# Expert loop of a two-block transformer kernel: the two high down passes as one 512-column matmul, its halves added by ScalarE and VectorE, and operand tiles placed 32 bytes apart modulo 64

## The chip, the cores and the metric

The kernel runs on one NeuronCore of a Trainium2 chip. The metric is the device time of one execution in microseconds (us). Three runs of the kernel before gave a median of 2825.68 us (2825.58 to 2825.96).

## What is computed

The reference is a network of two hybrid layers (recurrent, attention and state space mixers, then a product-key expert layer) followed by two layers of a second kind (retention, gating, cross attention, gated feed-forward). There are 256 tokens of width 1024. The change is mostly about the expert layer:

```python
def expert_block(args):
    xb, ib, gb = args
    a = jnp.einsum('thkd,td->thk', down[ib], xb).astype(jnp.float32)
    c = (gb * jax.nn.gelu(a)).astype(up.dtype)
    return jnp.einsum('thk,thkd->td', c, up[ib]).astype(x.dtype)
```

Each token picks 16 of 16384 experts for each of 8 heads. The kernel doesn't gather them: it multiplies all tokens with all experts' `down` rows, applies gelu, multiplies by a gate matrix that is zero where an expert isn't picked, and multiplies the result with all `up` rows.

## The kernel before

Products are made from float32 values in `float32r` form: each operand is split into a high part (a ScalarE copy that rounds) and a low part (VectorE: value minus high part), and a product is three passes on TensorE, high by high, high by low, low by high. A matmul takes a stationary operand of 128x128 and a moving operand of 128x256 or 128x512.

The experts of a layer are worked in 64 blocks of 256. For the first 32 ("held") blocks the activations are computed early (L1480 and L1462) and their output products are made in one long run (L1525). The other 32 blocks go through the expert loop: `pe.loop("peer", 15)` with two blocks in a turn (b = 0 and 1), and one block ahead of the loop and one behind it. Two layers make 64 calls of each function below.

- `act_in_parts(b)` (L1537) is the down product of a block: for 2 halves `j` of 128 experts and 8 slices `kc` of the width, three matmuls of 256 columns: (`down_hi`, `h_t_expert`), (`down_hi`, `h_t_lo`), (`down_lo`, `h_t_expert`), all into PSUM bank 4 + b, `j` in its left or right half. The `down` part is stationary and the token part moves. 48 matmuls a call.
- ScalarE's `gelu(b)` (L1173) reads that bank and writes the tile `gelu`. VectorE's `coef` (L2059) multiplies by the gates, ScalarE's `coef_high` (L1176) and VectorE's `coef_low` (L2063) split the product.
- `out_of_parts(b)` (L1547) is the up product: 24 matmuls of 512 columns; `coef` parts are stationary, `up` parts move.
- In the order of their queues, ScalarE does gelu, `down_hi` (L1134), `coef_hi`, `up_hi` (L1134); VectorE does `coef`, `coef_lo`, `down_lo` (L2030), `up_lo` (L2030). SyncE loads the next blocks into `ring` when `down_lo` and `up_lo` have been made.

TensorE's order in a turn is down product of block 1, up product of block 0, down product of block 0, up product of block 1. A down product of b waits for `down_lo` and for the last `gelu` of b (the bank is free then); an up product waits for `up_lo` and `coef_lo`. Behind the loop of a layer the last down product is followed by 18 matmuls of block 0 (`out_before`), and then `out_last` waits for `coef_lo_last1`. Ahead of the loop two down products follow each other, and the first up product waits for `coef_lo0`.

Other matmuls that the change touches by where their operands lie: L598 and L1480 and L2648 (256 columns), L607, L2666 and L2925 (512 columns). In the second block's L2666 the parts of a weight tile (`w_hi`, `ring_lo`) move and those of an activation (`h_t_hi` and `h_t_lo`, `ff_hi` and `ff_lo`, `mt_hi` and `mt_lo`) are stationary, in the order (hi, hi), (activation hi, weight lo), (activation lo, weight hi). By its loops L607 has 480 matmuls of 512 columns (five blocks of columns, 48 each, in two layers), L2925 has 192, and L2666 has 64 with `mt` in each of its three passes beside those with `h_t` and `ff`.

**Where tiles lie.** Tiles are allocated one behind another in each partition, so their places follow from their sizes. `x_res`, `h_t_lo`, `ring_lo` (over `ring`) and `h_t_expert` start at a multiple of 64 bytes. `hybrid_params` has 72 words (288 bytes), so every tile behind it, with all other matmul operands (`out_hi`, `out_lo`, `coef_hi`, `coef_lo`, `held_hi`, `held_lo`, `down_*`, `up_*`, `w_hi`, `ff_*`, `mt_*`, `h_t_hi`, `lead_x_*`), starts 32 bytes past one. Matmul operands start within a tile at steps of 512 bytes, so this is a property of the tile. Below, "at 0" and "at 32" name the two places, and two operands are "apart" if one is at 0 and the other at 32.

Of the kernel before, what the change touches and what calls it, by code (L numbers as in the profile page):

```python
# [8 lines left out]
ALU = mybir.AluOpType  # L9
ACT = mybir.ActivationFunctionType  # L10
AX = mybir.AxisListType
F32 = mybir.dt.float32
# [9 lines left out]
KD = D // P  # L22
DEPTH = 2
# [29 lines left out]
HELD = BLOCKS // 2  # L53
REACH = [(0, 0, 1, 16), (16, 1, 3, 8), (40, 4, 4, 4), (56, 8, 8, 1)]
# [278 lines left out]
def build(nc, dram, out, steps):  # L333
    ctx = ExitStack()
    with ctx:
# [19 lines left out]
        with nc.sbuf_tensor("h_t_expert", [P, KD, T], F32R) as HT_EXPERT:  # L355
            pass
# [12 lines left out]
        with ExitStack() as second:  # L369
            second.enter_context(nc.sbuf_tensor("before_ya", [P, 3 * 512], F32))  # L370
# [3 lines left out]
        KEYS = sb("keys", [P, P])  # L374
        with nc.sbuf_tensor("out_lo", [P, OUT_SLOTS, D], F32R) as OUT_LO:
            pass
# [8 lines left out]
        with nc.sbuf_tensor("arena", [P, 32768 + STAGES * GROUP * 64], F32) as ARENA:  # L385
            pass

        with ExitStack() as second:
# [6 lines left out]
            over("before_w", [P, 2 * KD * T], F32)  # L395
            W_HI = over("w_hi", [P, HI_SLOTS, CHUNK_SIZE])
            FF_HI, FF_LO = over("ff_hi", [P, KF, T]), over("ff_lo", [P, KF, T])
# [5 lines left out]
        with nc.sbuf_tensor("before_gate_hi", [P, 17 * 512], F32), nc.sbuf_tensor("gate_hi0", [P, D], F32R) as GATE_HI0, \  # L403
                nc.sbuf_tensor("lead_x_hi", [P, KD, T], F32R) as LEAD_X_HI, nc.sbuf_tensor("lead_x_lo", [P, KD, T], F32R) as LEAD_X_LO, \
                nc.sbuf_tensor("first_hi", [P, 2, D], F32R) as FIRST_HI:
            pass
        DOWN_HI, DOWN_LO = sb("down_hi", [P, 2, 2 * D], F32R), sb("down_lo", [P, 2, 2 * D], F32R)
        UP_HI, UP_LO = sb("up_hi", [P, 2, 2 * D], F32R), sb("up_lo", [P, 2, 2 * D], F32R)
        with nc.sbuf_tensor("held_hi", [P, HELD_SLOTS, 512], F32R) as HELD_HI:
            pass  # L410
        with nc.sbuf_tensor("gate_hi1", [P, D], F32R) as GATE_HI1, nc.sbuf_tensor("gate_hi2", [P, D], F32R) as GATE_HI2:
            pass
# [70 lines left out]
        for n in (8, 8, 4, 2, 2):  # L483
# [12 lines left out]
            after_scr, N_SPAR, KD * T, KD * T, KD * T, TT * D, HI_SLOTS * CHUNK_SIZE, N_Z3, 2 * T, TT * 1536,  # L496
# [212 lines left out]
        def late_stage(n):  # L709

            return 32768 + (n % STAGES if n >= STAGES else n - STAGES) * GROUP * 64
# [193 lines left out]
        def hybrid_scalar(a, l):  # L905
# [274 lines left out]
            with a.loop("peer", BLOCKS // 4 - 1):  # L1180
                a.e.wait_ge(*a.at("act_in0", back=1))
                a.e.wait_ge(*a.at("coef_lo0", back=1))
                gelu(0, "gelu0")
# [9 lines left out]
                a.e.wait_ge(*a.at("coef_lo1", back=1))  # L1193
                gelu(1, "gelu1")
# [9 lines left out]
            a.e.wait_ge(*a.at("coef_lo0"))  # L1204
            gelu(0, "gelu_last0")
# [7 lines left out]
            a.e.wait_ge(*a.at("coef_lo1"))  # L1213
            gelu(1, "gelu_last1")
# [3 lines left out]
        def hybrid_tensor(pe, l):  # L1218
# [249 lines left out]
            def passes_quarter(b, q):  # L1468
# [7 lines left out]
                for kc in range(4 * first, 4 * first + 4):  # L1476
                    o = slice(kc * P, (kc + 1) * P)
                    x_hi, x_lo = (LEAD_X_HI, LEAD_X_LO) if b < OWN_X else (HT_EXPERT, HT_LO)
# [1964 lines left out]
```

## Time and profile before

| | |
|---|---|
| median of 3 runs | 2825.68 us |
| the profiled execution | 2825.48 us |
| its span, first to last instruction | 2823.7 us |
| TensorE busy | 2803.2 us, 99% |
| weight loads busy | 2528.1 us, 90% |
| VectorE, ScalarE, GpSimd busy | 69%, 50%, 5% |
| granted TensorE clock | 0.999 of full speed |

Span and time differ by 1.8 us. A matmul's own duration in the profile overlaps with the next one's, because matmuls are pipelined; what a stream of them costs is the distance from start to start, or the length of a piece of the chain over its count.

### The profile page before, as it was taken

What the parts mean: (1) busy time and instruction counts of PE and PEld (TensorE: products, weight loads), DVE (VectorE), ACT (ScalarE), POOL (GpSimd) and SP (SyncE); (2) the same over time, 40 slices, a digit from 0 to 9 for tenths busy, and PEclk for the clock granted to TensorE, in tenths of its full rate; (3) what the DMA queues carried; (4) which work ended last, traced back from release to release, by engine and by line L of the source; (5) the groups of instructions that cost most, each with busy time, mean ns of one, the idle gap of its engine ahead of it and who ended that gap; (6) DMA issues with size and microseconds to landing.
All of it is one profiled execution on the core that took longest, in us unless ns stands there. A gap on an engine that the chain in (4) does not pass through costs nothing.

```text
span 2823.7 us, 45734 instructions
## 1 busy us (share of the span) xinstructions
PE 2803.2 (99%) x18566; PEld 2528.1 (90%) x18566; DVE 1943.8 (69%) x2882; ACT 1419.7 (50%) x1707; POOL 148.4 (5%) x145
## 2 busy tenths in 40 slices
PE   8999999999999999999999999999999999999998
PEld 7899998899999889999889999988899988888997
DVE  7889888655555788988865555576656556565664
ACT  6653554544444665355454444455455444545543
POOL 0033110000000003311000000000000000000000
PEclk9999999999999999999999999999999999999999
DMA  6344666855553534466685555465555656554663
GB/s 214 124 162 138 218 247 208 287 213 199 186 194 141 187 120 158 141 217 239 205 288 215 194 192 193 149 223 170 181 166 182 187 188 185 171 180 155 175 187 133
DMA packets 219570, 530.21 MB, mean 188 GB/s; under 512 B 13546, under 2 KB 87440, under 8 KB 208400
## 3 DMA queue, kind: packets, MB, share of 16 engines
q1 hardware_dynamic: 212944, 504.32, 54.2%
q0 software_dynamic: 6464, 23.61, 2.1%
q8 instruction: 116, 1.90, 0.3%
q14 instruction: 46, 0.38, 0.1%
HBM read 507.81 MB, written 20.06 MB: 187 GB/s over the span
## 4 chain that ended last, share of the span: by engine, by line
PE 98%; DVE 1%; DMA 1%; issue 0%; ACT 0%; SPq 0%; DVEq 0%
PE ps L2666 17%; PE ps L2648 13%; PE ps L1537 13%; PE ps L1547 12%; PE ps L1525 12%; PE ps L1480 11%; PE ps L607 4%; PE ps L598 4%; PE ps L1451 2%; PE ps L2925 2%; PE ps L1462 1%; PE ps L1255 1%; PE ps L2834 0%; PE ps L2818 0%; DMA ring<-in_peer_down 0%; PE ps L1367 0%
## 5 line engine op out<-in xcount | busy, mean ns | idle before, releaser
L2267 DVE TENSOR_TENSOR ring_lo<-ring,w_hi 128x1024 fp32r<-128x1024 f32 x320 | 388.2, 1224 | 243.0 <-ACT w_hi L2263 241.7
L2263 ACT ACTIVATE w_hi<-ring 128x1024 fp32r<-128x1024 f32 x320 | 335.2, 1056 | 236.1 <-PE ps L2666 169.0
L1537 PE MATMUL ps<-h_t_lo,down_hi 128*128 128x256 f32 x1024 | 288.2, 281 | 0.0
L1537 PE MATMUL ps<-h_t_expert,down_lo 128*128 128x256 f32 x1024 | 287.8, 281 | 0.0
L1537 PE MATMUL ps<-h_t_expert,down_hi 128*128 128x256 f32 x1024 | 286.8, 280 | 0.0
L2648 PE MATMUL ps<-h_t_lo,w_hi 128*128 128x256 f32 x928 | 260.7, 281 | 0.0
L2648 PE MATMUL ps<-h_t_hi,w_hi 128*128 128x256 f32 x928 | 259.4, 280 | 0.1
L2648 PE MATMUL ps<-h_t_hi,ring_lo 128*128 128x256 f32 x928 | 259.0, 279 | 0.0
L1143 ACT ACTIVATE out_hi<-ring 128x1024 fp32r<-128x1024 f32 x128 | 135.7, 1060 | 162.0 <-PE ps L1525 154.6
L2030 DVE TENSOR_TENSOR up_lo<-ring,up_hi 128x2048 fp32r<-128x2048 f32 x64 | 146.7, 2292 | 97.7 <-ACT up_hi L1134 97.7
L2023 DVE TENSOR_TENSOR out_lo<-ring,out_hi 128x1024 fp32r<-128x1024 f32 x128 | 156.6, 1224 | 77.1 <-ACT out_hi L1143 77.1
L1547 PE MATMUL ps<-up_hi,coef_hi 128*128 128x512 f32 x512 | 200.6, 392 | 0.0
L1547 PE MATMUL ps<-up_hi,coef_lo 128*128 128x512 f32 x512 | 199.9, 390 | 0.0
L1547 PE MATMUL ps<-up_lo,coef_hi 128*128 128x512 f32 x512 | 199.4, 390 | 0.0
L1525 PE MATMUL ps<-out_hi,held_hi 128*128 128x512 f32 x512 | 199.4, 389 | 0.0
L1525 PE MATMUL ps<-out_hi,held_lo 128*128 128x512 f32 x512 | 199.2, 389 | 0.0
L1525 PE MATMUL ps<-out_lo,held_hi 128*128 128x512 f32 x512 | 199.2, 389 | 0.0
L1134 ACT ACTIVATE up_hi<-ring 128x2048 fp32r<-128x2048 f32 x64 | 122.7, 1917 | 150.5 <-PE ps L1547 147.2
L1537 PEld LDWEIGHTS ps<-h_t_lo,down_hi 128*128 128x128 f32 x1024 | 193.0, 188 | 2.4
L1537 PEld LDWEIGHTS ps<-h_t_expert,down_hi 128*128 128x128 f32 x1024 | 192.5, 188 | 2.4
L1537 PEld LDWEIGHTS ps<-h_t_expert,down_lo 128*128 128x128 f32 x1024 | 193.3, 189 | 0.0
L2666 PE MATMUL ps<-w_hi,h_t_hi 128*128 128x512 f32 x448 | 180.3, 403 | 0.4 <-DVE ring_lo L2267 0.4
(532 smaller groups left out, 7403.5 us busy)
## 6 DMA issues: line engine op xcount, KB each, us to landing
ring<-in_peer_down SPq DMA_DIRECT2D x128, 1024.0 KB, 5.6
ring<-in_w_in SPq DMA_DIRECT2D x140, 512.0 KB, 3.7
ring<-in_peer_up SPq DMA_DIRECT2D x66, 1024.0 KB, 4.8
ring<-in_w SPq DMA_DIRECT2D x132, 512.0 KB, 3.8
ring<-in_peer_up SPq DMA_DIRECT2D x124, 512.0 KB, 4.2
late_gates<-arena POOLq DMA_DIRECT2D x64, 256.0 KB, 5.2
arena<-late_gates SPq DMA_DIRECT2D x16, 1024.0 KB, 6.4
ring<-in_w_out SPq DMA_DIRECT2D x16, 512.0 KB, 4.1
```

Of the source, the lines that this page charges most:

```text
L1134: a.e.activation(to[:, slot, :], raw(which, slot), ACT.Copy).then_inc(*a.count(name))
L1143: a.e.activation(OUT_HI[:, out_slot(b, j), :], up_raw(b, j), ACT.Copy).then_inc(*a.count(f"up_hi{b}{j}"))
L1480: m = pe.e.matmul(PS[:, act_bank(b), j * T:(j + 1) * T], w[:, o], x[:, kc, :], start=kc == 0 and n == 0, stop=kc == KD - 1 and n == 2)
L1525: m = pe.e.matmul(PS[:, 2 * t + half, :], x, w, start=b == 0 and j == 0 and n == 0, stop=False, skip_group_check=True)
L1537: m = pe.e.matmul(PS[:, 4 + b, j * T:(j + 1) * T], w[:, b, o], x[:, kc, :], start=kc == 0 and n == 0, stop=kc == KD - 1 and n == 2)
L1547: m = pe.e.matmul(PS[:, 2 * t + half, :], x[:, b, c], w[:, b, o], start=False, stop=last and n == 2, skip_group_check=True)
L2023: v.e.tensor_tensor(OUT_LO[:, out_slot(b, j), :], up_raw(b, j), OUT_HI[:, out_slot(b, j), :].bitcast(F32), ALU.subtract) \
L2030: v.e.tensor_tensor(lo[:, slot, :], raw(which, slot), hi[:, slot, :].bitcast(F32), ALU.subtract) \
L2263: a.e.activation(W_HI[:, g % HI_SLOTS, :], RAW[:, g % RAW_SLOTS, :], ACT.Copy).then_inc(*a.count(f"c{g}_hi"))
L2267: v.e.tensor_tensor(RAW_LO[:, g % RAW_SLOTS, :], RAW[:, g % RAW_SLOTS, :], W_HI[:, g % HI_SLOTS, :].bitcast(F32), ALU.subtract).then_inc(* ...
L2648: m = pe.e.matmul(PS[:, bank, c * T:(c + 1) * T], w[:, kc, c * P:(c + 1) * P], y[:, 4 * n + kc, :], start=n == 0 and c == 0 and kc == 0 an ...
L2666: m = pe.e.matmul(PS[:, bank + t, :], y[:, k0 + kc, o], w[:, kc, :], start=first and kc == 0 and i == 0, stop=last and kc == 1 and i == 2)
```

## The change

In the expert loop's down product the first two passes become one matmul. Its stationary operand is `down_hi`; its moving operand has 512 columns in two stretches, 256 of the tokens' low part and 256 of the high part, `TO_EXPERT` = 10656 words (42624 bytes) further on. So the left half of a bank gets `down_hi` by low, the right half `down_hi` by high, and the third pass (`down_lo` by high, 256 columns) is added in the right half. The two `j` need a bank each: banks 4 to 7 are used instead of 4 and 5. The halves are then added: ScalarE copies both left halves to `gelu` (`act_low`), VectorE adds the right halves to it (`act_sum`), and gelu runs in place in SBUF. TensorE waits for `act_sum` where it waited for gelu.

The second part is padding: 32-byte tiles (`before_ring`, `before_coef`, ...) and a few words more in others move operand tiles. Afterwards every token and activation operand (`h_t_lo`, `h_t_expert`, `h_t_hi`, `lead_x_*`, `held_*`, `coef_*`, `ff_*`, `mt_*`, `ya_hi`, `branch_*`) is at 0, and every weight operand (`ring_lo`, `out_*`, `gate_hi*`, `first_hi`, `down_*`, `up_*`, `w_hi`) at 32. `ring`, into which weights are loaded, is at 32 as well.

```diff
+TO_EXPERT = 10656
+LATE_AT = GATES + 512 * HELD + 16
...
+        with nc.sbuf_tensor("token_parts", [P, TO_EXPERT + KD * T], F32R) as TOKEN_PARTS:
+            pass
         HT_LO = sb("h_t_lo", [P, KD, T], F32R)
+        sb("before_ring", [P, 8])
...
-        with nc.sbuf_tensor("h_t_expert", [P, KD, T], F32R) as HT_EXPERT:
-            pass
+        sb("before_phase", [P, 8])
+        X_LO, HT_EXPERT = (TOKEN_PARTS[:, a:a + KD * T].rearrange("p (k t) -> p k t", t=T) for a in (0, TO_EXPERT))
...
         GELU = sb("gelu", [P, 2, 512])
+        sb("before_coef", [P, 8])
...
             def gelu(b, name):
-                a.e.activation(GELU[:, b, :], PS[:, 4 + b, :], ACT.Gelu_apprx_tanh).then_inc(*a.count(name))
+                a.e.activation(GELU[:, b, :], GELU[:, b, :], ACT.Gelu_apprx_tanh).then_inc(*a.count(name))
+
+            def act_low(b, name):
+                a.e.activation(GELU[:, b, :].rearrange("p (j t) -> p j t", j=2), PS[:, 4 + 2 * b:6 + 2 * b, 0:T], ACT.Copy) \
+                    .then_inc(*a.count(name))
...
                 a.e.wait_ge(*a.at("coef_lo0", back=1))
+                act_low(0, "act_low0")
+                a.e.wait_ge(*a.at("act_sum0"))
                 gelu(0, "gelu0")
...
-                        passes = ((DOWN_HI, HT_EXPERT), (DOWN_HI, HT_LO), (DOWN_LO, HT_EXPERT))
-                        for n, (w, x) in enumerate(passes):
-                            m = pe.e.matmul(PS[:, 4 + b, j * T:(j + 1) * T], w[:, b, o], x[:, kc, :],
-                                            start=kc == 0 and n == 0, stop=kc == KD - 1 and n == 2)
+                        first = TOKEN_PARTS[:, kc * T:kc * T + 1]
+                        low_and_high = bass.AP(tensor=first.tensor, offset=first.offset,
+                                               ap=[first.ap[0], [TO_EXPERT, 2], [1, T]])
+                        pe.e.matmul(PS[:, 4 + 2 * b + j, :], DOWN_HI[:, b, o], low_and_high,
+                                    start=kc == 0, stop=False, skip_group_check=True)
+                        m = pe.e.matmul(PS[:, 4 + 2 * b + j, T:2 * T], DOWN_LO[:, b, o], HT_EXPERT[:, kc, :],
+                                        start=False, stop=kc == KD - 1, skip_group_check=True)
...
-                pe.e.wait_ge(*pe.at("gelu1", back=1))
+                pe.e.wait_ge(*pe.at("act_sum1", back=1))
...
+            def act_sum(b, name):
+                banks = PS[:, 4 + 2 * b:6 + 2 * b, :]
+                act = GELU[:, b, :].rearrange("p (j t) -> p j t", j=2)
+                v.e.tensor_tensor(act, banks[:, :, T:2 * T], act, ALU.add).then_inc(*v.count(name))
+
             with v.loop("peer", BLOCKS // 4 - 1) as i:
                 for b in range(2):
+                    v.e.wait_ge(*v.at(f"act_low{b}"))
+                    act_sum(b, f"act_sum{b}")
                     v.e.wait_ge(*v.at(f"gelu{b}"))
```

## Rows read from the trace of the kernel before

**Rows 1.** The page: span, busy time by engine, the chain by engine and line.

```profile
span 2823.7 us, 45734 instructions
...
PE 2803.2 (99%) x18566; PEld 2528.1 (90%) x18566; DVE 1943.8 (69%) x2882; ACT 1419.7 (50%) x1707; POOL 148.4 (5%) x145
...
PE 98%; DVE 1%; DMA 1%; issue 0%; ACT 0%; SPq 0%; DVEq 0%
PE ps L2666 17%; PE ps L2648 13%; PE ps L1537 13%; PE ps L1547 12%; PE ps L1525 12%; PE ps L1480 11%; PE ps L607 4%; PE ps L598 4%; PE ps L1451 2%; PE ps L2925 2%; PE ps L1462 1%; PE ps L1255 1%; PE ps L2834 0%; PE ps L2818 0%; DMA ring<-in_peer_down 0%; PE ps L1367 0%
```

**Rows 2.** Page, groups by line of TensorE: busy us, mean ns, idle before.

```profile
L1537 PE MATMUL ps<-h_t_lo,down_hi 128*128 128x256 f32 x1024 | 288.2, 281 | 0.0
...
L1547 PE MATMUL ps<-up_hi,coef_hi 128*128 128x512 f32 x512 | 200.6, 392 | 0.0
...
L1537 PEld LDWEIGHTS ps<-h_t_lo,down_hi 128*128 128x128 f32 x1024 | 193.0, 188 | 2.4
...
L2666 PE MATMUL ps<-w_hi,h_t_hi 128*128 128x512 f32 x448 | 180.3, 403 | 0.4 <-DVE ring_lo L2267 0.4
...
L2666 PE MATMUL ps<-w_hi,ff_hi 128*128 128x512 f32 x176 | 69.9, 397 | 0.0
```

**Rows 3.** The chain in order of time: start us, length us, what, matmuls.

```profile
35.61 5.49 PE ps L607 x24
...
207.91 6.91 PE ps L1462 x32
...
403.54 174.15 PE ps L1525 x768
...
694.82 5.68 PE ps L1537 x48
700.50 5.47 PE ps L1547 x24
...
1887.25 22.20 PE ps L2666 x96
...
1995.58 19.42 PE ps L2925 x84
...
2638.23 115.89 PE ps L2648 x984
2754.12 61.33 PE ps L2666 x264
```

**Rows 4.** Timeline of ScalarE, then VectorE, half a turn: start, length, instruction.

```profile
700.62 0.60 ACT L1173 ACTIVATE gelu<-ps 128x512 f32<-128x512 f32 x1 [3.84 <-PE ps L1537]
...
711.76 0.60 ACT L1173 ACTIVATE gelu<-ps 128x512 f32<-128x512 f32 x1 [3.84 <-PE ps L1537]
...
703.56 0.69 DVE L2063 TENSOR_TENSOR coef_lo<-gelu,coef_hi 128x512 fp32r<-128x512 f32 x1 [1.08 <-ACT coef_hi L1176]
704.17 2.28 DVE L2030 TENSOR_TENSOR down_lo<-ring,down_hi 128x2048 fp32r<-128x2048 f32 x1
707.96 2.29 DVE L2030 TENSOR_TENSOR up_lo<-ring,up_hi 128x2048 fp32r<-128x2048 f32 x1 [1.50 <-ACT up_hi L1134]
```

**Rows 5.** Timeline behind the first layer's loop: ScalarE, VectorE, TensorE.

```profile
923.47 0.60 ACT L1173 ACTIVATE gelu<-ps 128x512 f32<-128x512 f32 x1 [3.70 <-PE ps L1537]
...
924.10 1.08 DVE L2059 TENSOR_TENSOR gelu<-gelu,arena 128x512 f32<-128x512 f32 x1 [2.00 <-ACT gelu L1173]
...
925.88 0.69 DVE L2063 TENSOR_TENSOR coef_lo<-gelu,coef_hi 128x512 fp32r<-128x512 f32 x1 [0.70 <-ACT coef_hi L1176]
...
928.94 0.69 DVE L757 TENSOR_TENSOR x_res<-ps,x_res 128x512 f32<-128x512 f32 x1 [0.72 <-PE ps L1547]
...
927.38 0.39 PE L1547 MATMUL ps<-up_hi,coef_hi 128*128 128x512 f32 x1
```

**Rows 6.** Timeline ahead of the first layer's loop: VectorE, TensorE.

```profile
586.59 0.69 DVE L2063 TENSOR_TENSOR coef_lo<-gelu,coef_hi 128x512 fp32r<-128x512 f32 x1 [1.08 <-ACT coef_hi L1176]
...
588.87 0.39 PE L1547 MATMUL ps<-up_hi,coef_hi 128*128 128x512 f32 x1
```

More of the change, by code:

```diff
@@ L369, in build @@
         with ExitStack() as second:
-            second.enter_context(nc.sbuf_tensor("before_ya", [P, 3 * 512], F32))
+            second.enter_context(nc.sbuf_tensor("before_ya", [P, 3 * 512 + 8], F32))
             YA_HI = second.enter_context(nc.sbuf_tensor("ya_hi", [P, 2, T], F32R))
         GELU = sb("gelu", [P, 2, 512])
+        sb("before_coef", [P, 8])
         COEF_HI, COEF_LO = sb("coef_hi", [P, 2, 512], F32R), sb("coef_lo", [P, 2, 512], F32R)
         KEYS = sb("keys", [P, P])
+        sb("behind_keys", [P, 8])
         with nc.sbuf_tensor("out_lo", [P, OUT_SLOTS, D], F32R) as OUT_LO:
@@ L384, in build @@
         HOT2 = (HOT2_EVEN, HOT2_ODD)
-        with nc.sbuf_tensor("arena", [P, 32768 + STAGES * GROUP * 64], F32) as ARENA:
+        sb("before_arena", [P, 8])
+        with nc.sbuf_tensor("arena", [P, LATE_AT + STAGES * GROUP * 64], F32) as ARENA:
             pass
@@ L394, in build @@
             MT_HI, MT_LO = over("mt_hi", [P, KD, T]), over("mt_lo", [P, KD, T])
-            over("before_w", [P, 2 * KD * T], F32)
+            over("before_w", [P, 2 * KD * T + 8], F32)
             W_HI = over("w_hi", [P, HI_SLOTS, CHUNK_SIZE])
+            over("behind_w", [P, 8], F32)
             FF_HI, FF_LO = over("ff_hi", [P, KF, T]), over("ff_lo", [P, KF, T])
@@ L402, in build @@
             pass
-        with nc.sbuf_tensor("before_gate_hi", [P, 17 * 512], F32), nc.sbuf_tensor("gate_hi0", [P, D], F32R) as GATE_HI0, \
+        with nc.sbuf_tensor("before_gate_hi", [P, 17 * 512 + 8], F32), nc.sbuf_tensor("gate_hi0", [P, D], F32R) as GATE_HI0, \
+                nc.sbuf_tensor("before_lead_x", [P, 8], F32), \
                 nc.sbuf_tensor("lead_x_hi", [P, KD, T], F32R) as LEAD_X_HI, nc.sbuf_tensor("lead_x_lo", [P, KD, T], F32R) as LEAD_X_LO, \
-                nc.sbuf_tensor("first_hi", [P, 2, D], F32R) as FIRST_HI:
+                \
+                nc.sbuf_tensor("before_first", [P, 8], F32), nc.sbuf_tensor("first_hi", [P, 2, D], F32R) as FIRST_HI:
             pass
+        sb("before_down", [P, 8])
         DOWN_HI, DOWN_LO = sb("down_hi", [P, 2, 2 * D], F32R), sb("down_lo", [P, 2, 2 * D], F32R)
         UP_HI, UP_LO = sb("up_hi", [P, 2, 2 * D], F32R), sb("up_lo", [P, 2, 2 * D], F32R)
+        with nc.sbuf_tensor("gate_hi1", [P, D], F32R) as GATE_HI1, nc.sbuf_tensor("gate_hi2", [P, D], F32R) as GATE_HI2:
+            pass
+        sb("before_h_t_hi", [P, 8])
         with nc.sbuf_tensor("held_hi", [P, HELD_SLOTS, 512], F32R) as HELD_HI:
-            pass
-        with nc.sbuf_tensor("gate_hi1", [P, D], F32R) as GATE_HI1, nc.sbuf_tensor("gate_hi2", [P, D], F32R) as GATE_HI2:
             pass
@@ L709, in late_stage @@
         def late_stage(n):
-            return 32768 + (n % STAGES if n >= STAGES else n - STAGES) * GROUP * 64
+            return LATE_AT + (n % STAGES if n >= STAGES else n - STAGES) * GROUP * 64
         def gates_of(n):
@@ L1193, in hybrid_scalar @@
                 a.e.wait_ge(*a.at("coef_lo1", back=1))
+                act_low(1, "act_low1")
+                a.e.wait_ge(*a.at("act_sum1"))
                 gelu(1, "gelu1")
@@ L1204, in hybrid_scalar @@
             a.e.wait_ge(*a.at("coef_lo0"))
+            act_low(0, "act_low_last0")
+            a.e.wait_ge(*a.at("act_sum_last0"))
             gelu(0, "gelu_last0")
@@ L1213, in hybrid_scalar @@
             a.e.wait_ge(*a.at("coef_lo1"))
+            act_low(1, "act_low_last1")
+            a.e.wait_ge(*a.at("act_sum_last1"))
             gelu(1, "gelu_last1")
@@ L1477, in passes_quarter @@
                     o = slice(kc * P, (kc + 1) * P)
-                    x_hi, x_lo = (LEAD_X_HI, LEAD_X_LO) if b < OWN_X else (HT_EXPERT, HT_LO)
+                    x_hi, x_lo = (LEAD_X_HI, LEAD_X_LO) if b < OWN_X else (HT_EXPERT, X_LO)
                     for n, (w, x) in enumerate(((hi, x_hi), (hi, x_lo), (lo, x_hi))):
@@ L1587, in hybrid_tensor @@
             pe.e.wait_ge(*pe.at("down_lo1"))
-            pe.e.wait_ge(*pe.at("gelu1"))
+            pe.e.wait_ge(*pe.at("act_sum1"))
             act_in_parts(1).then_inc(*pe.count("act_in_last"))
@@ L2076, in hybrid_vector @@
             for b in range(2):
+                v.e.wait_ge(*v.at(f"act_low_last{b}"))
+                act_sum(b, f"act_sum_last{b}")
                 v.e.wait_ge(*v.at(f"gelu_last{b}"))
```

6 lines of the change are left out of this document (3 added, 3 removed).

## The prediction

> **What bounds the kernel.** I read the page first. TensorE is busy for 99% of the span and the chain that ended last is 98% TensorE, with VectorE and DMA at 1% each [rows 1]. So time is the sum of TensorE's matmuls, start to start, and any other engine matters only where it makes TensorE wait. Next I read the groups by line to learn how many matmuls there are of each width [rows 2]. Their mean durations (281 ns, 392 ns) overlap and can't be added, so the price of a matmul comes from the chain in order of time: a piece's length over its count [rows 3].
>
> - A down product of the loop (L1537, 48 matmuls of 256 columns): 5.68 us, 118.2 ns each.
> - The second block's 256-column stream (L2648): 115.89 / 984 = 117.8 ns.
> - The held blocks' output (L1525, 512 columns): 174.15 / 768 = 226.8 ns. The loop's up product (L1547): 5.47 / 24 = 227.9 ns.
> - The other 512-column streams are dearer: L2666 22.20 / 96 = 231.3 ns and 61.33 / 264 = 232.3 ns, L2925 19.42 / 84 = 231.2 ns, L607 5.49 / 24 = 228.8 ns.
>
> At the granted clock, 2.4 GHz (0.999 of full speed), 256 columns are 106.7 ns and 512 columns 213.3 ns if one goes in per cycle. So each matmul pays something on top: 11.5 ns at 256 columns, 13.5 to 19 ns at 512. Both parts of the change are about this sum: one merges two small matmuls, so that it is paid once less; the other moves operands, which may change its size.
>
> **The merged passes.** A step of `kc` costs 3 x 118.2 = 354.6 ns now. Afterwards it is one 512-column and one 256-column matmul. The 512-column one with two stretches isn't in the trace. Its nearest rows are the 512-column streams, 226.8 to 232.3 ns. I take 226.8, because like L1525 the new stream has all moving operands at one place modulo 64 and all stationary ones at one place. With 118.2 for the third pass that is 345.0, so 9.6 ns are saved, in 16 steps of 64 calls: 1024 x 9.6 = 9.8 us. At 232.3 it would be 4.1 ns and 4.2 us. For the other end I take a matmul that shows almost no extra: L1462's pieces stream the same number of columns per 216 ns (6.91 / 32 [rows 3]; float32, two passes of 256 columns). At 216 the merged matmul would save 20.4 ns, 20.9 us in all. The Trainium skill (TensorE: Matmul & The Clock Gate, "Back-to-back issue gap") gives an isolated warm matmul N/2.4 + 2.5 ns, 109.2 and 215.8 ns here; an estimate by it is a saving of 2.6 ns a step, 2.7 us in all. The rows of L1537 and L1525 lie 9 and 11 ns over it, so the sum goes by the rows.
>
> **ScalarE and VectorE.** `act_low` is a ScalarE pass over 512 elements out of PSUM, as the gelu of before, 0.60 us [rows 4]. `act_sum` is a VectorE add of a PSUM and an SBUF operand of 512, as the one of L757, 0.69 us [rows 5]. With two handovers of 0.03 us each (the last gelu ends at 924.07, `coef` starts at 924.10 [rows 5]) the way from the down product to `coef_lo` gets 1.35 us longer. In the loop that is covered. Gelu starts at 700.62 and `coef_lo` ends at 704.25 [rows 4]; the up product that needs it starts one up and one down product later than the one running, at 700.50 + 5.47 + 5.67 = 711.6 [rows 3]. Of those 7.4 us, 1.35 go. ScalarE stands still while VectorE adds, and behind it are `down_hi`, `coef_hi` and `up_hi`; behind `act_sum` on VectorE are `coef`, `coef_lo`, `down_lo` and `up_lo`. `down_lo` ends at 706.45 and would end at about 707.8, `up_lo` at 710.25 and would end at about 710.3, since `up_hi`, which it waits for, still starts with the end of the up product. The next round begins with the next down product's end, at 711.6, so VectorE is just done, and TensorE needs these `down_lo` and `up_lo` no earlier than 717.1 and 722.8. SyncE's loads start when `down_lo` and `up_lo` are made, up to 1.4 us later, with a turn of 22 us to land in. TensorE's wait for the bank gets later by 0.7 us and is still over 10 us early. If this cover were gone it would be 64 x 1.35 = 86 us.
>
> It is gone at two places a layer. Behind the loop `coef_lo` ends at 926.57 and the matmul that waits for it starts at 927.38 [rows 5]: 0.81 us of room for 1.35, a stall of about 0.6 us. Ahead of the loop `coef_lo` ends at 587.28 and its matmul starts at 588.87 [rows 6]: 1.59 us, less 0.15 for the shorter second down product, against 1.35: about 0.1. Two layers: 1.4 us. The range for it is 0 to 3 us.
>
> **The padding.** It costs no instruction. Which operand pairs does it change? L1537 has tokens at 0 and `down_*` at 32 already: apart. L1525 and L1547 have both at 32, and will be apart. In L2666 and L2925 the moving operand alternates between 32 (`w_hi`) and 0 (`ring_lo`), the stationary one between 32 and 0 or stays; in L607 this holds for part of the blocks. Afterwards every stream has its moving operands at one place and its stationary ones at the other.
>
> What do rows say? Being apart doesn't take the extra away at 256 columns: L1537 is apart throughout and costs 118.2, the mixed L2648 117.8. At 512 columns no row has a stream that is apart throughout. What rows do show is that streams with all operands at one place (L1525, L1547: 226.8 and 227.9) are cheaper than those whose operands change place (L2666, L2925, L607: 228.8 to 232.3). So my likeliest case is that it is the alternation that costs, and that all 512-column streams come to 226.8. L2666 has 3 x (448 + 176 + 64) = 2064 matmuls (448 and 176 a pass [rows 2]; 64 with `mt`, 192 for L2925 and 480 for L607 by their loops). Gains: 2064 x 4.8 (from the mean of the two rows, 231.6) = 9.9 us, 192 x 4.4 = 0.8, 480 x 2.0 = 1.0, together 11.7 us.
>
> Sum: -9.8 + 1.4 - 11.7 = -20.1 us. From the profiled execution's 2825.48 us (span 2823.7 and 1.8 around it) that is 2805.4, from the median of the runs, 0.2 higher, 2805.6: **2805.5 us**. With the merged matmul and the streams 2 ns to either side: 2798 to 2814.
>
> **Rivals.**
> 1. *Apart is what frees the two reads from each other at 512 columns.* A weight load, 188 ns long in the profile [rows 2], runs beside each matmul; at 256 columns it may be the load that sets the pace, and then L1537 can't show it. For it: an extra of 13.5 to 19 ns that depends on place at all. Against it: L1537. If 216 ns (L1462's) were reached: L1525 and L1547 3072 x 11.3 = 34.7, L2666, L2925 and L607 2736 x 15.1 = 41.3, the merged matmul 20.9 instead of 9.8, and 1.4 back: -95.5, 2730 us. Halfway it is near 2768.
> 2. *Place changes nothing.* The differences between streams come from something else (PSUM banks, what other engines write). Then -9.8 + 1.4: 2817 us. The Trainium skill says so in effect (SBUF — State Buffer, "SBUF: two separate sides"): TensorE has ports of its own and never waits on another engine; its TensorE page gives the stationary and the moving operand a read port each ("Step-by-step: what each phase is for"). This trace neither proves nor refutes it; the 5 ns between L1525 and L2666 speak a little against it.
> 3. *Slower: apart costs more at 512 columns.* A third of L2666's `ff` matmuls have `ff_lo` (at 32) loaded while `ring_lo` (at 0) moves, and that piece is the dearest, 232.3. If apart throughout gave 236 ns (a third of the way beyond, by (232.3 - 226.8) x 3 the bound would be 243), L1525 and L1547 would lose 3072 x 9.2 = 28.3, L2666, L2925 and L607 2736 x 4.8 = 13.1, and the merged matmul would save nothing (354.2 against 354.6): 2868 us. At 232.3 throughout it is 3072 x 5.0 = 15.4 and 2736 x 1.1 = 3.0 lost, 4.2 - 1.4 won: 2841 us. It decides from 2 to 3 ns more on L1525, L1547 and the merged matmul.
> 4. *The jump between the two stretches costs.* If it costs 9.6 ns or more, the merging gives nothing: 2815 us with the padding's gain, 2827 without.
>
> **Chances.** Likeliest 0.38; rival 1 (or part of it) 0.27; rival 2 0.15; rival 3 0.13; rival 4 0.07. The line between change and no change is 0.2%, 5.7 us, about what a measurement of this kernel can tell. Faster takes the likeliest but for 0.02, rival 1, 0.10 of rival 2 and 0.03 of rival 4: 0.76. Same: 0.11. Slower: 0.13. The range must reach into rival 1 (its full size has perhaps half of its chance) and to the edge of rival 3: 2738 to 2832 us. The likeliest case alone is 2798 to 2814.
>
> **What would show it.** In the chain in order of time: the down product, now 32 matmuls, at 5.52 us (likeliest), 5.35 (rival 1), 5.6 or more (rivals 3 and 4); L1525's 768 matmuls at 174 us (likeliest, rival 2), 166 (rival 1), 178 or more (rival 3); L2666's 264 at 59.9 us (likeliest), 57 (rival 1), 61.3 (rival 2). In the timelines: `act_low` 0.60 us, `act_sum` 0.69 us, no idle TensorE in the loop, and about 0.6 us in front of the last up product's second part. The prediction is wrong if the price of a 512-column matmul with all operands apart isn't near 227 ns, which no row could tell me.

## The result, and the profile after

The changed kernel takes 2849.51 us (median of 4 runs, 2847.04 to 2851.4) against 2825.63 us before: ratio 1.0084, 95% interval 1.0066 to 1.0101. It is slower by 24 us, where 20 us less was forecast, and lies outside the range. The profiled execution took 2849.11 us with a span of 2847.3. TensorE's granted clock is 0.999 of full speed in both. The changed kernel's trace has one stretch of 3.4 us, from 1041.9 us on, at the lower of the two levels (1.2 instead of 2.4 GHz), with TensorE busy throughout; the kernel before has none before its last 5 us. At half speed 3.4 us can cost 1.7 us at most, so the clock doesn't explain the 24 us. A part of that stretch by windows: length, busy times of TensorE, its weight loads, VectorE, ScalarE and GpSimd, granted clock, DMA.

```profile
1042.00:1045.00 3.00, 3.00 (x14) 2.77 (x14) 1.24 (x4) 2.97 (x4) 0.00 (x0) 0.50 0.00 0
```

The page of the changed kernel: span, busy time by engine, the chain by engine [rows 1].

```profile
span 2847.3 us, 43934 instructions
...
PE 2827.9 (99%) x17542; PEld 2485.0 (87%) x17542; DVE 1988.4 (70%) x2946; ACT 1460.5 (51%) x1771; POOL 149.8 (5%) x145
...
PE 97%; DVE 1%; DMA 1%; ACT 0%; issue 0%; SPq 0%; DVEq 0%
```

TensorE has 1024 matmuls fewer and is still the bound. So single matmuls have become dearer, and the chain in order of time says which. The lines answer to [rows 3]: L1550 was L1525, L1575 was L1547, L2703 was L2666, L2685 was L2648.

```profile
404.69 179.21 PE ps L1550 x768
...
606.32 5.60 PE ps L1575 x24
...
617.56 5.60 PE ps L1575 x24
...
628.74 5.60 PE ps L1575 x24
...
1904.96 22.39 PE ps L2703 x96
...
2660.86 116.62 PE ps L2685 x984
2777.48 61.61 PE ps L2703 x264
```

Divide each by its count: 179.21 / 768, 5.60 / 24, 22.39 / 96 and 61.61 / 264 are all 233.2 to 233.4 ns. The padding did make these 512-column streams uniform, as forecast, but at 233.3 ns and not at 226.8. The half-turn is 11.24 or 11.18 us against 11.15, and less the up product's 5.60 it leaves 5.64 or 5.58 us for the 32 matmuls of the down product (5.67 or 5.68 for 48 before, 5.52 forecast).

The other engines went as forecast. Timelines of ScalarE and of VectorE in one half-turn [rows 4]: start, length, instruction.

```profile
707.38 0.60 ACT L1189 ACTIVATE gelu<-ps 128x512 f32<-128x512 f32 x1 [3.79 <-PE ps L1565]
```

```profile
708.01 0.69 DVE L2097 TENSOR_TENSOR gelu<-ps,gelu 128x512 f32<-128x512 f32 x1 [2.10 <-ACT gelu L1189]
```

The waits between 580 and 940 us (us in total, times, longest) hold one late place each for weight load and matmul in the whole loop of 32 half-turns. The wait of 0.1 us that was forecast ahead of the loop isn't among them.

```profile
PEld ps L1575 <- DVE coef_lo L2091: 0.9, 1, 0.9
PE ps L1575 <- DVE coef_lo L2091: 0.5, 1, 0.5
```

The chain behind the first layer's loop shows the place. Instead of TensorE the chain runs over ScalarE and VectorE for 4.7 us, and ends in the last up product's second part:

```profile
931.57 0.61 ACT gelu L1189
...
932.20 0.70 DVE gelu L2097
...
935.39 0.70 DVE coef_lo L2091
...
936.23 3.04 PE ps L1575 x12
```

TensorE's first part of the up product runs beside this; only the 0.5 us above is lost (0.6 was forecast).

Lengths of the stages, from the starts of TensorE's matmuls in each trace (us; L1525 and its like with 768 matmuls, the loop from the start of its first down product to the start of the last matmul of its last up product, the rest from there to the end of the span):

| kernel | to L1525 | L1525 | loop | to L1525 of layer 2 | L1525 | loop | rest |
|---|---|---|---|---|---|---|---|
| before | 403.4 | 174.2 | 357.4 | 388.1 | 174.4 | 357.4 | 968.8 |
| changed | 404.5 | 179.2 | 360.2 | 389.1 | 179.2 | 360.2 | 974.8 |

Of the 23.6 us of span, L1525 has 9.9, the two loops 5.6, the second block with what stands behind the loops 6.0, and the way to L1525 in both layers 2.1, of which the stretch at half clock may be a part.

### The profile page after: what moved, and what is told of

The parts are those of the page before. It is cut to its first block, busy times and chain, and to the rows that moved or that the text cites. A ratio compares the mean times of both kernels' runs of the same rounds, so it can differ in the third digit from the quotient of the medians.

```text
span 2847.3 us, 43934 instructions
## 1 busy us (share of the span) xinstructions
PE 2827.9 (99%) x17542; PEld 2485.0 (87%) x17542; DVE 1988.4 (70%) x2946; ACT 1460.5 (51%) x1771; POOL 149.8 (5%) x145
## 4 chain that ended last, share of the span: by engine, by line
PE 97%; DVE 1%; DMA 1%; ACT 0%; issue 0%; SPq 0%; DVEq 0%
PE ps L2703 17%; PE ps L2685 13%; PE ps L1550 13%; PE ps L1575 12%; PE ps L1505 11%; PE ps L1563 8%; PE ps L620 4%; PE ps L1565 4%; PE ps L611 4%; PE ps L1476 2%; PE ps L2962 2%; PE ps L1487 1%; PE ps L1280 1%; PE ps L2871 0%; PE ps L2855 0%; DMA ring<-in_peer_down 0%
## 5 line engine op out<-in xcount | busy, mean ns | idle before, releaser
L1563 PE MATMUL ps<-token_parts,down_hi 128*128 128x512 f32 x1024 | 362.0, 395 | 0.0
L1565 PE MATMUL ps<-token_parts,down_lo 128*128 128x256 f32 x1024 | 286.1, 279 | 0.0
L2685 PE MATMUL ps<-h_t_hi,w_hi 128*128 128x256 f32 x928 | 262.0, 282 | 0.1
L2685 PE MATMUL ps<-h_t_hi,ring_lo 128*128 128x256 f32 x928 | 261.2, 281 | 0.0
L2685 PE MATMUL ps<-h_t_lo,w_hi 128*128 128x256 f32 x928 | 259.9, 280 | 0.0
L1563 PEld LDWEIGHTS ps<-token_parts,down_hi 128*128 128x128 f32 x1024 | 192.2, 188 | 46.5
L1575 PE MATMUL ps<-up_hi,coef_hi 128*128 128x512 f32 x512 | 203.1, 397 | 1.0 <-DVE coef_lo L2091 1.0
L1550 PE MATMUL ps<-out_hi,held_lo 128*128 128x512 f32 x512 | 203.3, 397 | 0.0
L1550 PE MATMUL ps<-out_hi,held_hi 128*128 128x512 f32 x512 | 202.8, 396 | 0.0
L1575 PE MATMUL ps<-up_hi,coef_lo 128*128 128x512 f32 x512 | 202.7, 396 | 0.0
L1575 PE MATMUL ps<-up_lo,coef_hi 128*128 128x512 f32 x512 | 201.3, 393 | 0.0
L1550 PE MATMUL ps<-out_lo,held_hi 128*128 128x512 f32 x512 | 201.2, 393 | 0.0
L1565 PEld LDWEIGHTS ps<-token_parts,down_lo 128*128 128x128 f32 x1024 | 192.1, 188 | 2.6
L2703 PE MATMUL ps<-w_hi,h_t_hi 128*128 128x512 f32 x448 | 180.6, 403 | 0.2 <-DVE ring_lo L2304 0.2
L2703 PE MATMUL ps<-w_hi,h_t_lo 128*128 128x512 f32 x448 | 177.6, 397 | 0.0
L2703 PE MATMUL ps<-ring_lo,h_t_hi 128*128 128x512 f32 x448 | 175.8, 392 | 0.0
L2685 PEld LDWEIGHTS ps<-h_t_hi,w_hi 128*128 128x128 f32 x928 | 174.7, 188 | 0.7 <-DVE x_res L770 0.5
L2685 PEld LDWEIGHTS ps<-h_t_hi,ring_lo 128*128 128x128 f32 x928 | 174.8, 188 | 0.0
```

Of the source, the lines that this page charges most:

```text
L1550: m = pe.e.matmul(PS[:, 2 * t + half, :], x, w, start=b == 0 and j == 0 and n == 0, stop=False, skip_group_check=True)
L1563: pe.e.matmul(PS[:, 4 + 2 * b + j, :], DOWN_HI[:, b, o], low_and_high, start=kc == 0, stop=False, skip_group_check=True)
L1565: m = pe.e.matmul(PS[:, 4 + 2 * b + j, T:2 * T], DOWN_LO[:, b, o], HT_EXPERT[:, kc, :], start=False, stop=kc == KD - 1, skip_group_check=True)
L1575: m = pe.e.matmul(PS[:, 2 * t + half, :], x[:, b, c], w[:, b, o], start=False, stop=last and n == 2, skip_group_check=True)
L2685: m = pe.e.matmul(PS[:, bank, c * T:(c + 1) * T], w[:, kc, c * P:(c + 1) * P], y[:, 4 * n + kc, :], start=n == 0 and c == 0 and kc == 0 an ...
L2703: m = pe.e.matmul(PS[:, bank + t, :], y[:, k0 + kc, o], w[:, kc, :], start=first and kc == 0 and i == 0, stop=last and kc == 1 and i == 2)
```

## The experiments

Two questions: what does each half of the change do, and what sets the price of a 512-column matmul?

**Merging alone, padding alone.** `merge_only` is the changed kernel without its `before_*` tiles, so that all tiles stand where they stood; `pad_only` is the kernel before with those tiles and nothing merged.

```diff
# merge_only, against the changed kernel
-TO_EXPERT = 10656
+TO_EXPERT = 10640
...
-        sb("before_ring", [P, 8])
...
# pad_only, against the kernel before
+        sb("before_ring", [P, 8])
...
```

> The merged passes without any of the padding: token_parts lies where h_t_lo and h_t_expert lay (TO_EXPERT = 10640), every operand is placed as before. Theory (places cost it: a 512-column matmul takes 226.8 ns when moving and stationary operand are at one place modulo 64 and 233.3 ns when they are 32 bytes apart): the held blocks' output is back at 174 us for 768 matmuls and the up product at 5.47 us, while the merged down product stays at 5.62 us, since tokens (at 0) and down parts (at 32) are apart here too. Against before that is 64 x 0.05 = 3 us won and about 1 us of stalls: 2823 us. Rival (banks 4 to 7, the two more passes through PSUM, or the merging itself slow down all streams): the held output stays at 179 us and the time near 2845 to 2849 us.

> The padding alone: three passes of 256 columns and gelu out of PSUM as before, operands placed as in the changed kernel. Theory (places): held output 179.2 us, up product 5.60 us, the second block's 512-column streams 233 ns, down product 5.67 us, 2851 us, a little more than with the merging. Rival (the merging and its PSUM traffic cost it): 2825 us, held output 174 us.

`merge_only`: 2823.41 us, ratio 0.999 (0.9981 to 1.0). `pad_only`: 2851.88 us, ratio 1.0088 (1.0072 to 1.0105). The chains in order of time, first of `merge_only`:

```profile
403.42 174.13 PE ps L1541 x768
...
599.90 5.49 PE ps L1566 x24
...
2751.58 61.33 PE ps L2694 x264
```

and of `pad_only`:

```profile
406.76 179.21 PE ps L1536 x768
...
602.88 5.67 PE ps L1548 x48
608.54 5.59 PE ps L1558 x24
...
2780.80 61.61 PE ps L2677 x264
```

The two halves are separate: padding adds 26 us. Merging takes about 2 us away, which is at the edge of the noise in the whole time (the interval reaches 1.0); in the traces each loop is 0.6 us shorter (356.8 for 357.4). The unmerged down product doesn't feel the padding (5.67). With everything in its old place the merged one takes 11.10 - 5.49 = 5.61 us (half-turn from the same chain), 350.6 ns a step against 354.6.

**All operands at one place modulo 64.** If apart is dear, together should be cheap. `same_place_merged` is `merge_only` with 32 bytes before `h_t` and 32 behind the parameters, so that every float32r tile stands at 32 modulo 64.

```diff
+        sb("before_h_t", [P, 8])
         with nc.sbuf_tensor("h_t", [P, KD, T], F32) as HT:
...
+        sb("behind_params", [P, 8])
```

> The merging, and the opposite of the padding: 32 bytes ahead of h_t and 32 behind hybrid_params, so that every matmul operand of the whole kernel is at 32 modulo 64. Theory (places): all 512-column streams at 226.8 ns, those of the second block too (264 matmuls in 59.9 us instead of 61.3), the merged down product at 16 x 345 = 5.52 us: -11.7 - 9.8 + 1 = 2806 us. If only a change of place within a stream costs, or 64 bytes modulo 128 matter as well (w_hi and ff are 64 bytes from h_t_hi modulo 128), the second block stays at 231 to 233 ns and the time is about 2817 us. Rival (not places): 2845 us or more.

2826.19 us, ratio 1.0001 (0.9991 to 1.0011). Its chain in order of time:

```profile
405.42 174.15 PE ps L1543 x768
...
601.88 5.49 PE ps L1568 x24
...
1885.54 22.20 PE ps L2696 x96
...
2754.85 61.62 PE ps L2696 x264
```

L2696's matmuls are no cheaper than before, though all operands are together modulo 64. That theory fell: whatever the place counts in, it isn't 64 bytes.

**TensorE alone.** `streams` runs 96 matmuls each of several kinds with no other engine at work; `sweep` then goes over the distance, the start of the moving operand less that of the stationary one, in steps of 32 bytes. Both leave out the whole computation, as do `far` and `rhythms` below. One stretch of `sweep`:

```diff
+            for n in range(COUNT):
+                last = pe.matmul(PS[:, n % 8, 0:512], w(0, n), m(32, n), start=True, stop=True)
```

> TensorE alone, no other engine at work: streams of 96 float32r matmuls each, the moving operand 0, 4, 16, 32, 48, 64 and 96 bytes past the stationary one modulo 128 at 512 columns, 0, 16, 32 and 64 at 256 columns, both at 32, stationary at 32 with moving at 0, one of the two alternating, two stretches, and the merged pattern at 0 and 32 bytes. It leaves out the whole computation and writes x to the output. Theory (places): 226.7 ns at 0 bytes, 233.3 ns at 32 at 512 columns, in between when alternating; about 118 ns at 256 columns wherever they are; two stretches as one. Rival (what other engines read and write costs it): one price, near 216 ns, for all.

> TensorE alone again (the whole computation is left out, x is written to the output): the moving operand starts 0, 32, ... 480 bytes past the stationary one modulo 512, streams of 96 float32r matmuls each, at 512 columns and at 256; then distance 0 with both at 32 and both at 256 and a distance of 512; the merged pattern at 0 and 128; and four streams that add three matmuls into a bank as the kernel does, at distance 0 and 32, two of them with the up product's order of operands (stationary a, a, b, moving c, d, c). Theory A (distance modulo 64 alone sets the price): 0, 64, 128, ... at 226.7 ns, 32, 96, ... at 233.3 ns; but streams gave 232.4 at 128 and 228.8 at 320, so it is shaken. Theory B (the distance modulo 512 sets it, and 0 is the good one): 226.7 ns at 0 and 512 wherever both lie, 229 to 237 ns at all others. Theory C (the order of operands or the adding into one bank sets it): 226.7 ns only in the streams that add three into a bank, or only in those with the up product's order at distance 0, and 232 or more at distance 0 otherwise.

The chain of `streams`, four pieces: 512 columns at distance 128 modulo 256 bytes (L54), at 32 (L63), at 128, 32, 128 in turn (L81), and at 32 again with two stretches of 256 columns (L102).

```profile
46.77 22.31 PE ps L54 x96
...
114.21 22.40 PE ps L63 x96
...
248.19 22.19 PE ps L81 x96
...
360.17 22.40 PE ps L102 x96
```

L63 and L102 are 233.3 ns both: a jump between the stretches costs nothing here, and no other engine is needed for that price. L81 tests what the prediction had built on, that a change of place within a stream costs: 231.1 ns, against 232.4 (L54) and 233.3 for its parts alone. Here alternating was cheaper. The chain of `sweep`, 512 columns at distances 0, 32, 64 (L62 to L68) and 160 (L77), 256 (L86), 320 (L92), then 256 columns at 0 (L137) and at 192 (L155):

```profile
34.39 21.76 PE ps L62 x96
56.15 22.40 PE ps L65 x96
78.56 21.98 PE ps L68 x96
...
145.35 22.48 PE ps L77 x96
...
212.61 21.77 PE ps L86 x96
...
256.78 21.98 PE ps L92 x96
...
578.39 11.52 PE ps L137 x96
...
646.70 10.91 PE ps L155 x96
```

The pattern repeats after 256 bytes. 512 columns cost 226.7 ns at 0, 228.9 at 64, and 233.2 to 234.3 at the six other distances; 256 columns cost 113.3 ns at 192 and 117.4 to 120.0 elsewhere. Moving both operands together (by 32 or by 256 bytes, tried at distance 0) gave 21.81 and 21.79 us, so it is the distance that counts and not where both stand. This sorts the uniform 512-column streams of the full kernels too, by the addresses of their tiles. In the kernel before, `out_*` against `held_*` and `up_*` against `coef_*` stand at distance 0 modulo 256, the cheapest for 512 columns. In the changed kernel `out_*` stands at 96 or 160 from `held_*`, `up_*` at 96 from `coef_*`: 233.3. In `same_place_merged` both are back at 0: 226.8 and 228.8.

**Places chosen by the sweep.** `tokens192` moves only `h_t_lo` and `h_t_expert`, to 192 from `down_*`. `apart192` puts all weight and coefficient tiles at 192 modulo 256 and all activation tiles at 128, so that a 256-column matmul stands at 192, the expert products of 512 columns stay at 0, and the layers' come to 64. `apart192_merged` has these places and the merged down product.

```diff
# tokens192, against the kernel before
+        sb("before_tokens", [P, 24])
         with nc.sbuf_tensor("h_t", [P, KD, T], F32) as HT:
...
+        sb("before_ring", [P, 40])
...
+        sb("before_expert", [P, 8])
...
+        sb("before_params", [P, 56])
# apart192, against the kernel before (pads of 16, 24 or 48 words at a dozen tiles; `lower` and `hybrid_params` moved)
+        sb("before_phase", [P, 24])
+        sb("before_out", [P, 16])
+        sb("before_arena", [P, 48])
+        sb("before_down", [P, 16])
+        sb("before_h_t_hi", [P, 48])
...
```

> The kernel before, with the two token operands of the expert loop (h_t_lo, h_t_expert) moved so that each stands 192 bytes behind down_hi and down_lo modulo 256; every other tile keeps its place modulo 256, and nothing else is changed. THEORY (the price of a float32r matmul goes by the start of the moving operand less the start of the stationary one that is loaded beside it, modulo 256 bytes, in the full kernel as with TensorE alone): the 3072 matmuls of the down product go from 118.2 to 113.3 ns, L1537's own half-turn share from 32 steps... in short the half-turn from two starts apart 11.10-11.25 to about 11.0 us and the whole by 15.1 us; the lead's and the layers' matmuls that use the same tiles change places among 117 to 120 ns and give some 4 us of it back: by the sweep's prices, matmul by matmul, 10.7 us less in all, about 2815. RIVAL A (the sweep's low price at 192 holds only with TensorE alone, other engines' reads spoil it): 2826. RIVAL B (TensorE is not the bound of the loop at 113 ns, a subtraction or a weight load ends later): the down matmuls at 113.3 but waits in front of them, 2820 to 2826.

> The kernel before, unmerged, with every float32r tile placed for its pair: all tiles of weights and coefficients at 192 modulo 256, all tiles of activations at 128, so that a 256-column matmul (activations move, weights stand) has distance 192, the expert products of 512 columns stay at distance 0, and the layers' 512-column matmuls (weights move, activations stand) come to distance 64. No instruction is changed. THEORY (distance modulo 256): by the sweep's prices, matmul by matmul (15816 of them), 2506.8 us before against 2451.2: 55.6 us less, so about 2770 if TensorE stays the bound everywhere; where waits end later than the faster matmuls less is left, 2770 to 2790. Lines: the down product 113.3 ns, L1534's 768 at 174.1 us, the layers' 512-column matmuls 228.9 in place of 231 to 233. RIVAL A (prices hold only with TensorE alone): 2826. RIVAL B (the two changes that were timed show a bound elsewhere in the layers): the loop gains its 15 us and the rest little, 2805 to 2811.

> The same places with the merged down product of the change. THEORY (distance modulo 256): the merged matmul of 512 columns stands at distance 192 and costs 233.3 ns, the third pass 113.3: a step is 346.6 against 339.9 of three passes, 6.8 us more over 1024 steps, and 1.4 us of waits at the ends: 7 to 8 us over the unmerged kernel with these places, about 2778. RIVAL (merging saves 9.6 ns of each step whatever the places, as 3 x 118.2 against 226.8 + 118.2): 10 us under the unmerged kernel with these places.

`tokens192`: 2830.3 us, ratio 1.0015 (1.0006 to 1.0024), slower where 11 us less was expected. `apart192`: 2806.38 us, ratio 0.9929 (0.9915 to 0.9943), faster by 19.7 us where 55.6 was expected. `apart192_merged`: 2809.31 us, ratio 0.9942 (0.9928 to 0.9956). The chain of `tokens192`:

```profile
407.91 174.11 PE ps L1529 x768
...
609.86 5.65 PE ps L1541 x48
615.52 5.44 PE ps L1551 x24
...
2000.45 19.60 PE ps L2929 x84
...
2646.31 116.62 PE ps L2652 x984
```

and of `apart192`:

```profile
184.39 21.97 PE ps L1489 x192
...
397.86 174.27 PE ps L1534 x768
...
599.97 5.65 PE ps L1546 x48
...
1873.36 21.99 PE ps L2675 x96
2269.32 61.60 PE ps L2675 x264
...
2619.68 115.89 PE ps L2657 x984
```

What came out: the lead's matmuls (21.97 / 192 = 114.4 ns, in a stretch that took 23.05 before), and the layers' 512 columns with `h_t_*` (229.1). What didn't: the down product costs 117.7 ns at distance 192 in both kernels, the 984 of L2657 117.8, and L2675's 264 with `ff_*` 233.3 although they stand at 64. In `tokens192` the loops got 1.7 us shorter each, and the stages outside the loops and L1525, whose tiles but for the token parts had kept their places modulo 256, 12.2 us longer. Its profiled run is the slowest of its 11 (2833.97 us), and its trace has two stretches of 3.4 us at half clock outside the loops, of up to 1.7 us each. That leaves some 9 us that the clock doesn't explain. Streams whose distances hadn't changed took part: 84 matmuls of L2925 (here L2929) went from 19.42 to 19.60 us, while the loop's up product (L1551), at distance 0 as before, went from 5.47 to 5.44 us. So a price by distance, though read exactly with TensorE alone, doesn't add up in a kernel. The merged product has no edge there: its loop takes 357.4 us against 355.7 of the unmerged.

**Why 117.8 and not 113.3?** `far` repeats the matmuls at the very addresses of `apart192` and the kernel before, and in their order; `rhythms` asks whether it matters what ran before. A single matmul and a stretch of `rhythms`:

```diff
+            # 256 columns, 64
+            for n in range(1):
+                last = pe.matmul(PS[:, n % 8, 0:256], w(20480, n), m(28736, n), start=True, stop=True, skip_group_check=True)
+            # 256 columns, 192
+            for n in range(96):
+                last = pe.matmul(PS[:, n % 8, 0:256], w(20480, n), m(28864, n), start=True, stop=True, skip_group_check=True)
```

> TensorE alone, as in the sweep; the whole computation is left out, the output is a copy of the input. One tile over nearly all of SBUF, so that operands can stand at the very addresses of the full kernels; 96 matmuls for each case, in the sweep's order (weights 512 bytes on, moving 2048 bytes on each time), in the down product's order (three passes over two weights and two token parts, 24 matmuls added into one place) and in the layers' order. Asked: why 256 columns at distance 192 cost 117.8 ns in the full kernel and 113.3 in the sweep, and why 512 columns at 64 modulo 256 cost 229.1 ns with h_t_hi and 233.3 with ff_hi. THEORY A (the order of the operands: the price goes by the moving operand against the weights loaded next to it, and by how far both go on between matmuls, so a tile used twice changes it): down order near 117.8 like down order at the real addresses, sweep order at the real addresses 113.3. THEORY B (the distance counts in a longer period than 256, or the address itself counts): down order near 113.3, both orders at the real addresses 117.8, and one of the distances 192 + 2^k shows it. THEORY C (many matmuls added into one place cost more than one each into its own): 24 into a place 117.8 in both orders, one each 113.3. For 512 columns: A: 64 and 320 alike in the layers' order, B: 229 against 233. Merged: at the addresses of the changed kernel 233.3 + 117.8 = 351.1 ns for a pair, at those of the kernel before 3.4 to 7 ns less.

> TensorE alone, the computation left out as in the sweep. The run before showed the same 256-column matmuls at distance 192 at 113.3 ns and, after a stretch at other addresses, at 117.8, with no return. THEORY (at some distances TensorE can settle into more than one steady rhythm, and what ran just before chooses): 96 matmuls at 192 come to 113.3 ns after a stretch at 160 and to 117.8 after some others; a single matmul at another distance in the midst of a stretch is enough to switch it; 512 columns at distance 0 stay at 226.7 whatever came before. RIVAL (113.3 needed low addresses or a fresh start, not the stretch before): always the same price at 192 here. Then a loop of 24 up-product matmuls at distance 0 and 48 down-product matmuls, with the two token parts at each of 8 by 8 places: with both at 192 117.8 ns a down matmul, as in the full kernel with those places; if some pair of places gives 113.3 to 115, it could take 8 to 14 us from the expert loops; if none does, the loop's down product is at its floor of 117.4 to 117.8.

In `far` the matmuls share one line, so the prices are taken from their starts in the trace, in the order in which they ran:

```
256 columns, distance 192                        ns
near, sweep's order, a bank each                 113.3
near, sweep's order, 24 into a place             113.3
near, down product's order, a bank each          113.3
near, down product's order, 24 into a place      113.3
addresses of apart192, down order, a bank each   117.8
addresses of apart192, sweep's order             117.8
512 bytes to 120 KB further on (9 cases)         117.8
near, sweep's tiles again, weights kept thrice   117.8
near, both operands always the same              117.8
... (down order at 0 to 160)                     117.4 to 120.0
near, down product's order, 24 into a place      113.3
```

The fourth and the last row are the same kind of matmul at the same distance, and so is all that lies between at 117.8: neither the order nor the sums make the difference, and near addresses can cost 117.8 too. The price rose with the step to the far addresses, at an unchanged distance, and stayed until stretches at other distances had run.

`far` has two more results. At the kernel before's own addresses, where L2666's distances change from pass to pass, TensorE alone takes 231.1 ns with `h_t_*` (192, 96, 96 in turn; 231.3 in the kernel) and 232.2 with `ff_*` (0, 160, 0; 232.3 in the kernel). `sweep`'s prices for these distances have means of 233.3 and 229.2. So a stream whose distance changes has a price of its own, here below or above that of its parts, and no other engine is needed for it. And a merged matmul with its third pass takes 346.7 ns at distance 0, 349.8 at the addresses of `merge_only` (350.6 there) and 353.3 at 192. (The case meant for the changed kernel stands 32 bytes beside its true place and says nothing of it.)

`rhythms` shows the choice. Its chain: 96 matmuls at 192 after 96 at 160 (L91), at 0 (L97), after 512 columns at 0 (L133), and after single matmuls at 64 (L175) and 128 (L187):

```profile
89.75 11.30 PE ps L91 x96
...
112.57 10.90 PE ps L97 x96
...
256.50 11.31 PE ps L133 x96
...
400.96 10.90 PE ps L169 x96
411.97 11.30 PE ps L175 x96
...
434.82 10.90 PE ps L187 x96
...
479.27 21.80 PE ps L208 x96
```

One matmul at 64 between L169 and L175 turns 113.5 ns (10.90 / 96) into 117.8 for the next 96, and one at 128 ahead of L187 turns it back. So at distance 192 TensorE has two steady rhythms, and what ran before chooses, not by its distance alone: after 96 at 160 it was the dear one here (L91) and the cheap one in `sweep` (L155). After 512 columns at 0, the up product's kind, it was the dear one, behind 96 of them (L133) and behind a single one. 512 columns at 0 have only one in all that was tried (L208: 227.1 with the way in). Other distances have two prices as well: 256 columns at 32 cost 117.8 ns in `sweep` and 116.7 in `rhythms`, at 160 they cost 117.4 and 118.7, and 512 columns at 128 cost 233.3 and 232.4. In the loop of an up and a down product with the token parts at 8 by 8 places, the down matmul cost 116.7 to 120.7 ns: no pair of places reaches 113.3, and the 118.2 of the kernel before is within 2 ns of the best.

## Why the prediction was wrong

- **What bounds the kernel** was right: TensorE, matmul after matmul, before and after.
- **The failed step is the padding's term**: "it is the alternation that costs, and that all 512-column streams come to 226.8", 11.7 us gained. In its place: uniform, but at 233.3 ns, about what `sweep` has at the distances 96, 160 and 224 modulo 256 bytes (233.2 to 234.3), and L1525 and L1547, which stood at distance 0, pushed off it. Alternation as such isn't what costs: in `streams` it made matmuls cheaper (231.1). In L2666 with `ff_*`, where distance 0 takes turns with 160, it was dearer than the mean of its parts. From the rows: 1536 x 6.6 ns on L1525 = 10.1 us and 1536 x 5.4 on L1547 = 8.3. The stages of `pad_only` show the same: L1525 9.9 us longer, the loops 7.1, the second block 6.0 and the way to L1525 4.0 (up to 1.7 of it one stretch of 3.4 us at half clock), together 26.9 us of span. The two streams that I took as the model for "all together" were cheap for being at distance 0 modulo 256, which the modulo 64 of the diff hid from me: `same_place_merged` shows that together modulo 64 isn't enough for L2666.
- **The merged matmul was mis-sized**: 9.6 ns a step forecast, 4.0 measured in `merge_only` (350.6), 4.1 us in place of 9.8. With 118.2 for the third pass its 512-column part costs 232.4, nearer 233 than 226.8. That no stretch of it stands at distance 0 (96 and 160 in `merge_only`, 160 and 32 in the changed kernel) is the likely reason, since in `far` the pair cost 346.7 ns at 0 and 349.8 at `merge_only`'s addresses. It isn't shown: in `sweep`, where both matmuls of a pair take their weights from one tile, the pair at distance 0 cost 353.1.
- **The stalls** were right. In `merge_only` a loop is 0.65 us shorter; the down products give 512 x 4.0 = 2.05, the up products cost 768 x 0.85 = 0.65 more (5.49 for 5.47), which leaves about 0.75 us of stalls a layer, 0.7 forecast.
- **Rival 3 is what happened**: apart costs more at 512 columns. At 232.3 throughout it gave 2841 us, decided "from 2 to 3 ns more on L1525, L1547 and the merged matmul", and L1525's 768 at 178 us or more; measured 179.21 and 2849.5. It had a chance of 0.13. (Its other sum, 2868 us at 236 ns, has 3072 x 9.2; from L1547's own 227.9 it is 26.6 us instead of 28.3.) The rest of the way is 233.3 for 232.3, and the 256-column pieces, which the rival left alone (L2648's 984 went from 115.89 to 116.62). Its cause, apart modulo 64, isn't the one found: `sweep` has 233.3 ns at 128, which is together modulo 64. That these paddings came to dear distances modulo 256 was chance.
- **Rival 1** (apart frees the reads) is refuted by the same rows. **Rival 2** (place changes nothing) is refuted by `pad_only`, where no instruction changed, and by `sweep`: 226.7 to 234.3 ns with TensorE alone. The Trainium skill (TensorE: Matmul & The Clock Gate, "Step-by-step: what each phase is for") says that loading the next weights takes no read bandwidth from the running matmul; with a load beside every matmul the sweep shows 3% between two distances of the same operands, which that sentence doesn't account for. That the two reads meet in SBUF is a guess; no run shows it. **Rival 4** (the jump costs) is refuted by `streams` at distance 32: 233.3 with one stretch and with two.

What stays open: why a distance costs what it does, which rhythm a stretch in a full kernel falls into, and hence why L2675's `ff` matmuls cost 233.3 in `apart192` where `far` gave 228.9 at the same addresses.

## What to carry to other kernels

Before padding tiles or moving operands, write down for the costly streams the distance of the moving from the stationary operand modulo 256 bytes, and the price in the chain; for 512 columns of float32r keep or seek 0 for every pass of the stream, and don't trust a smaller modulus. A price measured in one stream belongs to its distance and to what runs before it: don't carry it to another stream whose distance you haven't worked out, and run a layout as a whole rather than adding up prices. Merging passes of a matmul that streams back to back saves only the extra of one matmul less what the wider one pays more, here 4 ns in 355. Before adding up stages of two traces, look whether one of them has a stretch at the lower clock that the mean of 0.999 doesn't show.

## What the runs showed of the hardware

- The extra of a float32r matmul with a weight load beside it (over 106.7 and 213.3 ns) goes by the distance of the operands modulo 256 bytes: 13.4 ns at 0 and 20.0 at most other distances for 512 columns, 6.6 to 13.3 ns for 256 columns, with no other engine at work.
- At one distance (192, 256 columns) there are two steady rhythms, 113.3 and 117.8 ns, and a single matmul at another distance can switch between them; two prices also showed at 32 and 160 (256 columns) and at 128 (512 columns).
- A stream whose distance changes from matmul to matmul has a price of its own: 231.1 ns for 128, 32, 128 in turn, below both parts (232.4, 233.3), and 232.2 for 0, 160, 0, above their mean (229.2).
- At the lower clock the extra is gone: in the stretch at 0.50 from 1041.9 us on in the changed kernel, 256-column matmuls start 213 ns apart, twice the 106.7 ns that their columns take at the full clock.
- Layout alone, without one instruction changed, moved this kernel from 2825.6 to 2806.4 us and to 2851.9 us.
